# A hybrid S5, attention and MoE block on one core: the front reordered, q and k normed apart, fewer matmuls in attention

## What is computed

```
hn = rmsnorm(x);  u, q, k, v = split(hn @ w_in)          # four times 512 columns
y_ssm = S5(u): state 64, 32 groups of 16 channels;  gelu(y + d*u);  y * sigmoid(y @ w_glu + b)
y_att = stick-breaking attention, 8 heads of 64, on rmsnorm(q), rmsnorm(k), v
h = x + concat(rmsnorm(y_ssm), rmsnorm(y_att)) @ w_out
out = h + shared_expert(rmsnorm(h)) + top-8-of-64 routed experts(rmsnorm(h))
```

## Time and profile before

| | us |
|---|---|
| runs | 617.65, 618.33, 618.50 |
| median of the runs | 618.33 |
| the profiled execution, by the runs' clock | 617.45 |
| its span in the trace | 615.7 |
| PE busy | 581.4 (94%) |
| DVE busy | 253.0 (41%) |
| ACT busy | 133.7 (22%) |
| POOL busy | 17.7 (3%) |
| mean DMA rate over the span | 365 GB/s |

### The profile page before, as it was taken

One profiled execution on the slowest core, in us unless ns is written; L12 is line 12 of the kernel. 1 busy time (PEld: TensorE's weight loads), 2 busy tenths in 40 slices (PEclk: granted clock), 3 DMA queues, 4 the chain that ended last, 5 costly groups with the idle time before them and its releaser, 6 DMA issues.

```text
span 615.7 us, 9969 instructions
## 1 busy us (share of the span) xinstructions
PE 581.4 (94%) x3974; PEld 264.6 (43%) x3974; DVE 253.0 (41%) x676; ACT 133.7 (22%) x289; POOL 17.7 (3%) x48
## 2 busy tenths in 40 slices
PE   4999989999999998999989999999999999999795
PEld 1455456656544433334434434343434434343322
DVE  7999981447752332232332322313222314123122
ACT  3342664203322111102101212020202112110101
POOL 5000021000000000000000000000000000000000
PEclk9999999999999999999999999999999999999989
DMA  8934455994499999999999999999999999999995
GB/s 346 433 141 160 87 141 221 430 390 177 136 324 424 426 422 394 426 431 420 429 422 426 428 423 427 422 425 425 424 426 422 429 422 426 423 429 423 423 409 206
DMA packets 29246, 224.99 MB, mean 365 GB/s; under 512 B 6656, under 2 KB 7168, under 8 KB 11776
## 3 DMA queue, kind: packets, MB, share of 16 engines
q1 hardware_dynamic: 29024, 224.22, 89.2%
q10 hardware_dynamic: 176, 0.13, 0.1%
HBM read 222.11 MB, written 1.05 MB: 362 GB/s over the span
## 4 chain that ended last, share of the span: by engine, by line
PE 74%; DVE 13%; DMA 9%; issue 2%; ACT 1%; SPq 1%; POOL 0%; DVEq 0%; ACTq 0%
PE bank L696 71%; DVE ring L1441 5%; DMA wreg<-in_e_w 4%; DMA ring<-in_e_w 4%; DVE reg_c L1441 3%; PE bank L1081 2%; DMA ring<-in_x_turned 1%; DVE wreg L1441 1%; DVE small L1441 1%; SPq L392 1%; PE bank L1108 1%; DVE ring L1447 0%; DVE reg_ab L1441 0%; DVE small L1586 0%; ACT wreg L1216 0%
## 5 line engine op out<-in xcount | busy, mean ns | idle before, releaser
L696 PE MATMUL bank<-ring,wreg 128*32 128x512 f32 (+2 forms) x1272 | 249.9, 595 | 2.9 <-DMA wreg<-in_e_w 2.3
L696 PE MATMUL bank<-wreg 128*32 128x512 f32 (+5 forms) x445 | 145.4, 587 | 0.1
L696 PEld LDWEIGHTS bank<-ring,wreg 128*32 128x32 f32 (+1 forms) x1272 | 71.2, 119 | 110.2 <-issue 106.6
L1441 DVE TENSOR_TENSOR wreg<-wreg,bank 128x256 f32<-128x256 f32 x28 | 11.8, 422 | 165.1 <-ACT wreg L1368 165.1
L696 PE MATMUL bank<-wreg,reg_ab 128*128 128x512 f32 (+1 forms) x192 | 76.6, 546 | 0.0
L696 PE MATMUL bank<-reg_ab,wreg 128*64 128x512 f32 (+2 forms) x192 | 70.8, 559 | 0.9 <-DVE reg_ab L1681 0.9
L696 PE MATMUL bank<-reg_d 128*128 128x512 f32 (+1 forms) x140 | 63.5, 592 | 3.1 <-DVE reg_d L1880 3.1
L696 PE MATMUL bank<-side,wreg 128*32 128x512 f32 (+2 forms) x150 | 59.2, 590 | 3.3 <-DMA ring<-in_e_w 3.3
L1441 DVE TENSOR_TENSOR acc<-acc,bank 128x512 f32<-128x512 f32 (+1 forms) x70 | 47.1, 673 | 29.8 <-PE bank L696 28.6
L1216 ACT ACTIVATE reg_d<-bank 128x512 f32<-128x512 f32 (+2 forms) x47 | 22.2, 473 | 163.3 <-PE bank L696 99.5
L696 PEld LDWEIGHTS bank<-wreg 128*32 128x32 f32 (+4 forms) x445 | 39.1, 123 | 37.5 <-issue 36.4
(11 more groups left out here) (193 smaller groups left out, 379.5 us busy)
## 6 DMA issues: line engine op xcount, KB each, us to landing
ring<-in_e_w SPq DMA_DIRECT2D x36, 2048.0 KB, 21.3
ring<-in_e_w SPq DMA_DIRECT2D x46, 1024.0 KB, 20.4
wreg<-in_e_w SPq DMA_DIRECT2D x14, 2048.0 KB, 21.5
reg_ab<-in_e_w SPq DMA_DIRECT2D x8, 2048.0 KB, 21.3
wreg<-in_e_w SPq DMA_DIRECT2D x12, 1024.0 KB, 15.5
side<-in_e_w SPq DMA_DIRECT2D x9, 1024.0 KB, 16.6
wreg<-in_w_in SPq DMA_DIRECT2D x3, 2048.0 KB, 22.9
wreg<-in_w_out SPq DMA_DIRECT2D x1, 4096.0 KB, 14.0
```

The lines of the kernel that those rows point to most:

```text
L696: return nc.tensor.matmul(out_, lhsT, rhs, start=start, stop=stop, **kw)
L1441: return nc.vector.tensor_tensor(out_, a, b, op)
```

## The change

On SP, u's columns arrive in four pieces of two k each (before bc), q's in two halves with x_chunks between, and the diagonal's vector moves here from ACT. ACT issues x turned, in four pieces. ACT scales all of xT, in four pairs around the exponents and the sines, makes all of hnT, writes the zeroth columns of Et and G (plain copies of Bbar and C) and clears Tm. POOL computes the powers, rho's broadcast (decay), Kdiag and its addition to K. DVE's products for Et have 7 columns and for G 8; `token_scales` and u's transpose (`turn_u`) sit in G's. q and k are normed by `norm_heads(0)` and `norm_heads(1)`, the second behind scan_turn; scan pieces 0 and 1 stand ahead of the first clamp. PE begins with 18 matmuls on a constant, takes u with k as outer loop, splits the second half of k around V's transposes, and turns q's heads after five and k's after seven of the eight steps of project_v(0). ACT's evac_v(0) goes behind the head copies. add_logs is two matmuls for three. DVE adds the four squares into one (`add_squares`), and PE sums one group of columns for four.

```diff
-            sp.dma_start(xT, I["x_turned"].rearrange("p (k t) -> p k t", k=KT)).then_inc(S["xT_in"], 16)
             wi = I["w_in"].rearrange("n p (k c) -> n p k c", k=KT)
-            sp.dma_start(w_in[:, 0, 0:KT // 2], wi[0, :, 0:KT // 2]).then_inc(S["wu_lo"], 16)
-            sp.dma_start(w_in[:, 0, KT // 2:KT], wi[0, :, KT // 2:KT]).then_inc(S["wu_hi"], 16)
+            for n in range(KT // 2):
+                ks = slice(2 * n, 2 * n + 2)
+                sp.dma_start(w_in[:, 0, ks], wi[0, :, ks]).then_inc(wu_in[n], 16)
             sp.dma_start(bc_in, I["bc"]).then_inc(S["bc_in"], 16)
+            sp.dma_start(w_in[:, 1, 0:KT // 2], wi[1, :, 0:KT // 2]).then_inc(S["wq_lo"], 16)
             sp.dma_start(acc[:, :], I["x_chunks"]).then_inc(S["x_in"], 16)
+            sp.dma_start(w_in[:, 1, KT // 2:KT], wi[1, :, KT // 2:KT]).then_inc(S["wq_hi"], 16)
             sp.dma_start(x_nat, I["x_rows"]).then_inc(S["nat_in"], 16)
-            for n in (1, 2, 3):
-                sp.dma_start(w_in[:, n], wi[n]).then_inc(S[("", "wq_in", "wk_in", "wv_in")[n]], 16)
+            sp.dma_start(w_in[:, 2], wi[2]).then_inc(S["wk_in"], 16)
+            sp.dma_start(dT[0:H, :], I["d_skip"]).then_inc(S["d_in"], 16)
+            sp.dma_start(w_in[:, 3], wi[3]).then_inc(S["wv_in"], 16)
...
-            sp.wait_ge(S["consts_ready"], 2)
+            sp.wait_ge(S["zeroth"], 3)
...
-            nc.gpsimd.memset(Tm, 0.0).then_inc(S["consts_ready"], 1)
...
-            for k in range(KT):
-                pool.wait_ge(S["xC_odd"] if k % 2 else S["xC_even"], k // 2 + 1)
-                nc.gpsimd.tensor_copy(chunked(hnT[:, k, :]),
-                                      hnC[:, k, :].rearrange("p (a q c) -> p a q c", a=2, q=4)).then_inc(S["xT_ready"], 1)
+            def cmul(outs, x, y, tmps, done=step):
+                for o, (i, j) in zip(tmps, ((0, 0), (1, 1), (0, 1))):
+                    nc.gpsimd.tensor_tensor(o, x[i], y[j], ALU.mult)
+                step(nc.gpsimd.tensor_tensor(tmps[3], x[1], y[0], ALU.mult))
+                nc.gpsimd.tensor_tensor(outs[0], tmps[0], tmps[1], ALU.subtract)
+                done(nc.gpsimd.tensor_tensor(outs[1], tmps[2], tmps[3], ALU.add))
+            nc.gpsimd.memset(PW[0][:, 0, :], 1.0)
+            nc.gpsimd.memset(PW[1][:, 0, :], 0.0)
+            pool.wait_ge(S["lb_ready"], 1)
+            nc.gpsimd.tensor_copy(PW[0][:, 1, :], lbr)
+            step(nc.gpsimd.tensor_copy(PW[1][:, 1, :], lbi))
+            for have in (1, 2, 4):
+                by = [PW[i][:, have:have + 1, :].to_broadcast([128, have, PR]) for i in range(2)]
+                tw = [power_tmp[i][:, 0:have * PR].rearrange("p (k r) -> p k r", k=have) for i in range(4)]
+                cmul([PW[i][:, have + 1:2 * have + 1, :] for i in range(2)],
+                     [PW[i][:, 1:have + 1, :] for i in range(2)], by, tw,
+                     step if have < 4 else lambda ins: ins.then_inc(S["PW_ready"], 1))
+            pool.wait_ge(S["V_done"], 2)
+            decay = scan_t[6].rearrange("p (r c) -> p r c", r=PR)
+            step(nc.gpsimd.tensor_copy(decay, rho.unsqueeze(2).to_broadcast([128, PR, C])))
+            nc.gpsimd.memset(decay[:, :, 0:1], 0.0).then_inc(S["turns_ready"], 1)
+            pool.wait_ge(S["d_in"], 16)
+            step(nc.gpsimd.tensor_tensor(Kdiag, ident[0:H, 0:H].unsqueeze(1).to_broadcast([H, G, H]),
+                                         dT[0:H, :].unsqueeze(2).to_broadcast([H, G, H]), ALU.mult))
+            pool.wait_ge(S["K_evac"], 8)
+            nc.gpsimd.tensor_tensor(Kv[:, :, 0:H], Kv[:, :, 0:H], Kdiag, ALU.add).then_inc(S["diag_ready"], 1)
...
+            pe.wait_ge(S["ones_ready"], 1)
+            for _ in range(N_WARM):
+                mm(ps[7][:, 0:128], negones, negones)
+            for k in range(KT):
+                if k % 2 == 0:
+                    pe.wait_ge(wu_in[k // 2], 16)
+                pe.wait_ge(S["xC_ready"], k + 1)
+                for a in range(2):
                     last = mm(ps[a][:, :], hnC[:, k, 128 * a:128 * a + 128], w_in[:, 0, k, :], k == 0, k == KT - 1)
...
-            project_qk(1, (0, 1))
+            project_qk(1, 0)
+            project_qk(1, 1)
...
-            project_qk(2, (1,))
+            project_qk(2, 1, range(0, 4))
...
+            project_qk(2, 1, range(4, KT))
+            pe.wait_ge(S["s5_ready"], 1)
+            pe.wait_ge(S["zeroth"], 2)
+            pe.wait_ge(S["s5_ready"], 3)
...
-            project_v(0)
-            pe.wait_ge(S["qk_normed"], 2)
+            def turn_heads(n):
+                pe.wait_ge(S["qk_normed"], 2 * n + 2)
+                for pair in range(2):
+                    for m in range(2):
+                        for a in range(2):
+                            c0 = 512 * n + 128 * (2 * pair + m)
+                            last = nc.tensor.transpose(ps[2 + 2 * n + pair][:, 256 * m + 128 * a:256 * m + 128 * a + 128],
+                                                       qk[:, a, c0:c0 + 128], ident[:, :])
+                    last.then_inc(S["qkT_done"], 1)
+            project_v(0, range(0, 5))
             pe.wait_ge(S["K_evac"], 8)
...
+            turn_heads(0)
+            project_v(0, range(5, KT - 1))
+            turn_heads(1)
+            project_v(0, range(KT - 1, KT))
...
-                mm(z[:, 0:256], negtri[:, :], Lm[:, 0:256], False, False, skip_group_check=True)
-                mm(z[:, 128:256], negones[:, :], Lm[:, 256:384], False, False, skip_group_check=True)
-                mm(z[:, 256:384], negtri[:, :], Lm[:, 256:384], False, True, skip_group_check=True).then_inc(S["zi_done"], 1)
+                mm(z[:, 0:384], negtri[:, :], Lm[:, 0:384], False, False, skip_group_check=True)
+                mm(z[:, 128:256], negones[:, :], Lm[:, 256:384], False, True, skip_group_check=True).then_inc(S["zi_done"], 1)
...
+            pe.wait_ge(S["qkT_act"], 3)
+            scores_of_pair(0)
             pe.wait_ge(S["qkT_act"], 4)
-            scores_of_pair(0)
             scores_of_pair(1)
...
+                pe.wait_ge(S["sq_added"], added)
                 for a in range(2):
-                    last = mm(ps[7][:, col + a:col + a + 1], sq[:, m, 128 * a:128 * a + 128], ones_col, m == 0 and a == 0, m == 3 and a == 1,
+                    last = mm(ps[7][:, col + a:col + a + 1], sq[:, 0, 128 * a:128 * a + 128], ones_col, a == 0, a == 1,
...
-                            sums_of_squares(sqa, 2, k)
                     last.then_inc(S["opa_done"], 1)
+                    if a == 0 and hf == 0:
+                        sums_of_squares(sqa, 2, 1)
...
+            for n in range(KT // 2):
+                act.dma_start(xT[:, 2 * n:2 * n + 2], x_turned[:, 2 * n:2 * n + 2]).then_inc(xT_in[n], 16)
             act.wait_ge(S["params_in"], 16)
             nc.scalar.activation(ls, ls, ACT.Exp).then_inc(S["step_ready"], 1)
-            act.wait_ge(S["a_ready"], 1)
+            def scale_x(n):
+                act.wait_ge(xT_in[n], 16)
+                for k in (2 * n, 2 * n + 1):
+                    copy(hnC[:, k, :], xT[:, k, :], scale=g_mix[:, k:k + 1]).then_inc(S["xC_ready"], 1)
+            scale_x(0)
+            act.wait_ge(S["angles_ready"], 1)
             nc.scalar.activation(mag, mag, ACT.Exp)
             nc.scalar.activation(rho, rho, ACT.Exp)
-            act.wait_ge(S["xT_in"], 16)
-            for k in range(1, KT, 2):
...
+            act.wait_ge(S["angles_ready"], 2)
             nc.scalar.activation(sinv, th, ACT.Sin)
             nc.scalar.activation(cosv, th, ACT.Sin, scale=0.5).then_inc(S["exps_ready"], 1)
+            scale_x(1)
+            scale_x(2)
+            scale_x(3)
+            act.wait_ge(S["xC_ready"], KT)
+            for k in range(KT):
+                copy(chunked(hnT[:, k, :]), hnC[:, k, :].rearrange("p (a q c) -> p a q c", a=2, q=4)).then_inc(S["xT_ready"], 1)
+            act.wait_ge(S["s5_ready"], 1)
+            copy(EtV[0][:, :, L - 1, :], Bbar[0])
+            copy(EtV[1][:, :, L - 1, :], Bbar[1]).then_inc(S["zeroth"], 1)
+            copy(GmV[0][:, :, 0, :], Ct[0])
+            copy(GmV[1][:, :, 0, :], Ct[1], scale=-1.0).then_inc(S["zeroth"], 1)
+            copy(Tm, ones_col.to_broadcast([128, G * 128]), scale=0.0).then_inc(S["zeroth"], 1)
...
+            for i in range(4):
+                act.wait_ge(S["qkT_done"], i + 1)
+                t, g = ((qT, gq), (kT, gk))[i // 2]
+                m = 2 * (i % 2)
+                copy(t[:, m:m + 2, :], ps[2 + i][:, :].rearrange("p (m t) -> p m t", m=2), scale=g).then_inc(S["qkT_act"], 1)
             evac_v(0)
...
-            dve.wait_ge(S["xT_in"], 16)
-            for k in range(0, KT, 2):
-                ts(hnC[:, k, :], xT[:, k, :], g_mix[:, k:k + 1], ALU.mult).then_inc(S["xC_even"], 1)
...
-            for have in (1, 2, 4):
-                by = [PW[i][:, have:have + 1, :].to_broadcast([128, have, PR]) for i in range(2)]
-                tw = [big[i][:, 0:have * PR].rearrange("p (k r) -> p k r", k=have) for i in range(4)]
```

(58 more changed lines are left out.)

119 lines of the change are left out of this document (44 added, 75 removed).

## The result

The changed kernel takes 616.72 us (median of 12 runs, 614.19 to 619.1) against 618.4 for the kernel before on the same chip (617.16 to 620.09): the ratio is 0.997, 95% interval 0.9958 to 0.9982. It is faster, by 1.7 us, where 6.5 were forecast. The profiled execution took 616.59 with a span of 614.6; before, that was 617.45 and 615.7.

The account below looks back on a forecast made before the run. TensorE was taken to bound the kernel (74% of the chain), behind a VectorE chain in the first 75 us. Front 1.2, attention 2.5 and sums of squares 2.8 gave 6.5 us: median 611.8, range 608.8 to 615.8.

Parts of the forecast that it names:

- The slower rival: Front: GpSimd's powers take 16 us, Et starts 9.2 late, the kernel is 2.7 slower at 621.0; chance 0.06.
- where I had put 1.8: Rotations: GpSimd's copy and diagonal product hold DVE up by 1.8 us, between 0 and 2.9.
- The attention stage: Up to 101.59 us: shorter PE waits for weights, mask and scan, plus 0.8 from add_logs, save 2.5 us.
- the sums: Sums of squares in two projections: one column group for four saves PE 1.4 us each, 2.8 together.
- PE stands at 66 [...] waits 3.5 for k. Then 0.95 of transposes and one step of v, 0.86: scores at 71.4.: Before attention: PE waits 3.5 us for k's norm at 69.5, then starts scores at 71.4 against 72.22.
- where I had put 3.9 down to it: Front: with the warm-up, u ends at 21.6 against 25.5; that 3.9 us becomes PE's wait for k.
- its DMA lands [...] 12.1.: Front: bc's load, near 12.5 before, lands at 12.1 because the stream begins 0.4 us earlier.
- the 0.7 of contention: Front: GpSimd's powers cost DVE 0.7 us through the shared port, so Et starts at 15.0, not 14.3.
- a saving ahead of 170 us moves the whole expert stage by the same amount.: Expert stage, 170 to 590 us: loads follow PE's freed buffers, so any earlier saving is kept to the end.
- eight add_logs lose one of three matmuls, 0.1 each: 0.8.: Attention stage: one matmul fewer in each of eight add_logs saves 0.8 us of the stage's 2.5.
- -1.2 forecast for the first logs: End of the front: the first logs of head 0 start at 76.6, 1.2 us earlier.
- the gain stops at attention: Rival: k's norm 2.5 us later than said, scores at 73.9, gain only 4.0, time 614.3; chance 0.20.

Follow-up runs that it names:

- e1_fill: Changed kernel plus 22 matmuls of a constant in PE's wait for k's norm; 614.02 us, 0.9937 of the kernel before.
- e7_bc_first: Changed kernel with only the DMA of b and c moved ahead of the last two of u's pieces; 612.8 us, 0.9921 of the kernel before.
- The control: The changed kernel run again, unaltered, beside the kernel before on another chip; 615.53 us, 0.9952 of the kernel before.
- e3_no_warm: Changed kernel without its 18 warm-up matmuls ahead of u; 614.74 us, 0.9952 of the kernel before.
- e6_best: Changed kernel with k's norm before scan_turn, scan pieces 0 and 1 back between attention's heads, and bc's load before u's last two pieces; 609.91 us, 0.9871.
- e4_squares: Kernel before plus only the matmul savings: squares added on DVE, one column group for four, two add_logs matmuls for three; 615.74 us, 0.9961.
- e5_pieces_back: Changed kernel with k's norm before scan_turn and scan pieces 0 and 1 back between attention's heads; 613.77 us, 0.9927 of the kernel before.
- e8_after_again: The changed kernel unaltered, repeated as the control on another chip; 615.53 us, 0.9952 of the kernel before.
- e2_k_first: Changed kernel with k's norm ahead of scan_turn on DVE; 614.85 us, 0.9956 of the kernel before.

## Why the prediction was wrong, point by point

**What held.** The sign, and most sizes. PE's u took the 32 matmuls from 7.41 on at the full rate and q's followed at 21.24 (21.6 said). The powers took GpSimd from 7.71 to 12.85: 5.1 us against 5 (ready 13.2). The slower rival, that they hold Et up, is out: DVE waits for bc, not for them. From Et's start to G's end it is 45.28-16.15 = 29.1 (28.9 said); x_rows' squares end at 25.96 (26 said) and the scales don't wait. q's norm takes 5.1 from the rotations' end (4.95 said), k's 5.05. GpSimd's copy and diagonal product (47.95 to 49.8) hold DVE's small products up: the six of 16 columns that took 0.43 and 0.26 before take 0.85 and 1.14, so 1.3 where I had put 1.8. The attention stage gives 2.1 (2.5 said), the sums 2.7 (2.8 said).

**What failed, in the order of its size.**

1. *"PE stands at 66 [...] waits 3.5 for k. Then 0.95 of transposes and one step of v, 0.86: scores at 71.4."* The wait was priced as its length alone. After it the same work took 1.97, 1.92 for two records of v and 2.47 for the scores, at 1.2 GHz. From k's transposes to the logs it is 6.93 us with the clock up, in `e1_fill` and in `e7_bc_first` alike, and 9.55 in the changed kernel: 2.62 for the clock. The control had 8.68 and `e3_no_warm` 8.45, so the price was 1.5 to 2.6. With the clock up, my step was right: I had 7.1 from k's norm to the logs. The Trainium skill, "TensorE: Matmul & The Clock Gate" (HAM oscillation), warns that waits of PE in mid-kernel bring the slower clock on the work behind them; the trace agrees, with 1.97 against 1.09 for the same eight transposes. I had weighed the clock for the start alone, where the change speeds it up, and never for the hole that this speed-up makes. The warm-up gives PE 2.4 us of head start, by `e3_no_warm`, where I had put 3.9 down to it; those 2.4 went into that wait of 5.2.

2. *"its DMA lands [...] 12.1."* It landed at 13.79, and 14.8 in the control. I took 0.4 off the old landing time of 12.5. But SP now issues bc later, at 3.69 instead of 2.69, since the four pieces of u take 2.38 us to issue; and from issue to landing it is 10.1, in the control 11.4, where it was 9.8. The same megabytes lie ahead of bc as before, but they moved more slowly: between 3 and 6 us the DMA engines were as busy (0.96 against 0.97) and moved 280 GB/s instead of 385, from 6 to 9 us 381 instead of 421. What the change did there was to cut the loads of x and u into smaller pieces on two queues; that this is the cause is argued, for no run puts the pieces back. DVE's 4.01 of idle time there is where the front's chain hangs on a transfer. It cost 1.15 at Et (16.15 against 15.0; the 0.7 of contention that I had put there did not come, since the powers were over). That DVE was through with lambda_bar at 9.88 and not at 10.8, as I had said, bought nothing behind this wait. k's norm was late by about the same, 70.68 against 69.5.

3. *"a saving ahead of 170 us moves the whole expert stage by the same amount."* In this pair of traces it did not: -2.29 at 145 us is -1.02 at 536. The wait is in PE's timeline, at the same place in all runs, first after and then in `e7_bc_first`; it was 0.43 before:

```profile
313.50 0.63 PE L728 MATMUL bank<-ring,wreg 128*32 128x512 f32 x3 [1.40 <-DMA wreg<-in_e_w]
```

```profile
308.72 0.63 PE L729 MATMUL bank<-ring,wreg 128*32 128x512 f32 x3 [1.06 <-DMA wreg<-in_e_w]
```

Here PE arrives at an expert's weights before they have landed, in a stretch where the DMA engines are full (share 1.00 from 300 to 317 us). SP issues that load 2.0 earlier than before, at 299.36, but it takes 14.00 us instead of 13.02. Being early is not what lengthens it: the load took 12.82 in `e6_best`, which is 8.9 ahead there, 12.91 in `e3_no_warm` and 13.66 in `e7_bc_first`. By 536 us `e3_no_warm`, `e4_squares` and `e6_best` had kept all of their lead or all but 0.1; `e5_pieces_back` had given back 0.5, `e8_after_again` 1.2, `e7_bc_first` 1.4, `e1_fill` 2.2 (it has a new wait of 0.98 for weights at 327.84) and `e2_k_first` 2.8. Each is one execution. By the medians the changed kernel keeps 1.7 of its 2.3. So the step holds in some executions and not in others; it is a small part of the miss, and what decides is not shown.

4. *"eight add_logs lose one of three matmuls, 0.1 each: 0.8."* Worth 0.05 in `e4_squares`. The three had 256, 128 and 128 output columns, the two have 384 and 128: the same 512, so only an instruction went. The stage's 2.1 came from waits instead: the mask's 0.43 and the scan's 0.74 are gone, the one for ACT's weights is 0.58 instead of 1.00, and the first row of the logs takes 1.90 instead of 2.17; that makes 1.86, and 0.2 is unassigned.

By the numbers, for the traced execution: -1.2 forecast for the first logs, +1.2 for bc's chain and +2.6 for the clock give +2.6; measured +2.46. With the stage (-2.1) and the sums (-2.7) that is -2.3 at 145 us, and with 1.2 given back by the end, -1.1. In the trace of `e7_bc_first`, with the two causes gone, the shift at 145 us is -6.9 where the prediction's sum had 6.5, and the median time is 612.8 where it had 611.8. There is some luck in that: bc landed 0.9 earlier there than the prediction had it, and in three of the six runs the clock did fall somewhere.

The rival "the gain stops at attention" had the right place, and its scores at 73.9 were near the 74.35 measured. But it wanted k's norm 2.5 late, which was 1.2 late, and looked for the cause on DVE and ACT alone; the rest came from PE's clock, which no rival had. Its 614.3 too is below the measured value.

## What to carry to other kernels

Price a wait of TensorE together with what stands behind it: where it idles for some microseconds, look at the granted clock of the next windows, and compare one form of matmul before and after. Speeding up TensorE's work ahead of such a wait, by a warm-up for instance, only lengthens it; order the late engine's queue by what TensorE wants next, or give TensorE something to do. Where a chain starts with a transfer, work out anew when it is issued and when it lands, for 2.1 us hung on that here. And a single trace shows where time goes, but a shift of a microsecond late in a long kernel needs the runs beside it.
